# Attention stage of a hybrid encoder layer: bias tables made on chip from distances, an identity made on chip, a store cut into pairs, delta loads moved between stores

## What is computed

```
proj = rmsnorm(x) @ w_in                  # split in two halves of columns by the kernel
A: gated delta rule in chunks of 64 tokens, both directions; needs the inverse of
   I + lower (64 x 64 per chunk and head), whose 16 x 16 diagonal blocks are inverted first
B: windowed attention, 12 heads of 64 in 3 groups with dilation f = 1, 4, 16:
   scores[q, k] = q.k / 8 - slope[head] * |k - q| * f    where |k - q| <= 64 and in range
   scores[q, k] = -1e30                                  elsewhere
   then softmax and the weighted sum of v
x = x + w_out(gates of A and B);  x = x + 16 experts of SwiGLU;  y = rmsnorm(x)
```

## Time and profile before

| what | us |
|---|---|
| median of three runs | 2660.21 |
| the profiled execution, its own time | 2656.95 |
| its span in the trace | 2654.8 |
| token projection (first load to the last store's issue) | 483.8 to 924.0 |
| attention (first load to the last rows) | 931.8 to 1076.8 |
| delta rule, first load | 1090.1 |

### The profile page before, as it was taken

The page is one execution under the profiler, slowest core; times in us unless marked ns, Lnnn a source line. Parts: engine busy times, 40 slices in busy tenths (PEclk is TensorE's granted clock), DMA queues, the critical chain, the costliest instruction groups (busy, mean ns, idle before and its releaser), DMA issues. The chain is left out here.

```text
span 2654.8 us, 48695 instructions
## 1 busy us (share of the span) xinstructions
PE 2342.1 (88%) x20450; PEld 2093.9 (79%) x20450; DVE 1354.3 (51%) x1673; ACT 1076.3 (41%) x1584; POOL 380.7 (14%) x375
## 2 busy tenths in 40 slices
PE   3988899799999979698767999659999999999992
PEld 2766688689999868698763555349999999999992
DVE  4445411125454358233226543467777777777772
ACT  3555511011111048111126553136666666666662
POOL 0000000000000038454423220000001000100000
PEclk7999999899999979799988999869999999999996
DMA  3233331238666496554634431447777777777754
GB/s 113 56 83 83 91 133 73 77 108 252 208 193 181 135 248 175 151 138 130 218 115 149 142 126 66 158 150 275 270 247 275 270 258 267 262 264 268 259 163 176
DMA packets 180105, 465.10 MB, mean 175 GB/s; under 512 B 63312, under 2 KB 108016, under 8 KB 152128
## 3 DMA queue, kind: packets, MB, share of 16 engines
q1 hardware_dynamic: 166560, 414.51, 47.4%
q0 software_dynamic: 13344, 47.67, 6.4%
HBM read 363.76 MB, written 102.26 MB: 176 GB/s over the span
## 5 line engine op out<-in xcount | busy, mean ns | idle before, releaser
L78 DVE TENSOR_TENSOR ex_w_rest<-weights,ex_w_rounded 128x2048 fp32r<-128x2048 f32 x192 | 439.4, 2289 | 208.5 <-ACT ex_w_rounded L2286 206.7
L2286 ACT CAST ex_w_rounded<-weights 128x2048 fp32r<-128x2048 f32 x192 | 366.7, 1911 | 30.3 <-PEq L48 30.3
L85 PE MATMUL tk_acc<-tk_w_rounded,normed 128*128 128x336 f32 x800 | 257.9, 322 | 19.2 <-DVE tk_w_rest L78 19.2
L2180 PE MATMUL ex_g_acc<-ex_xt,ex_w_rounded 128*128 128x320 f32 x1024 | 272.4, 350 | 1.4 <-issue 1.4
L2180 PE MATMUL ex_u_acc<-ex_xt,ex_w_rounded 128*128 128x320 f32 x1024 | 271.0, 349 | 0.0
L85 PE MATMUL tk_acc<-tk_w_rounded,normed_rest 128*128 128x336 f32 x800 | 255.4, 319 | 0.0
L85 PE MATMUL tk_acc<-tk_w_rest,normed 128*128 128x336 f32 x800 | 255.1, 319 | 0.0
L2181 PE MATMUL ex_g_acc<-ex_xt,ex_w_rest 128*128 128x160 f32 x1024 | 242.8, 237 | 0.0
L2181 PE MATMUL ex_u_acc<-ex_xt,ex_w_rest 128*128 128x160 f32 x1024 | 241.6, 236 | 0.0
L2181 PEld LDWEIGHTS ex_g_acc<-ex_xt,ex_w_rest 128*128 128x128 f32 x1024 | 197.6, 193 | 0.0
L2181 PEld LDWEIGHTS ex_u_acc<-ex_xt,ex_w_rest 128*128 128x128 f32 x1024 | 195.9, 191 | 0.0
(11 more groups left out here) (291 smaller groups left out, 5126.8 us busy)
## 6 DMA issues: line engine op xcount, KB each, us to landing
weights<-in_w_expert SPq DMA_DIRECT2D x192, 1024.0 KB, 5.2
proj_tok<-tk_stage SPq DMA_DIRECT2D x10, 1680.0 KB, 8.3
laq<-sc_laq SPq DMA_DIRECT2D x20, 768.0 KB, 4.1
dl_la<-laq SPq DMA_DIRECT2D x20, 768.0 KB, 5.0
tk_w<-in_w_tok SPq DMA_DIRECT2D x10, 1344.0 KB, 6.3
ch_w<-in_w_ch SPq DMA_DIRECT2D x24, 512.0 KB, 4.0
sc_rows<-rows SPq DMA_DIRECT2D x40, 256.0 KB, 6.2
sc_qk<-qkv_ch SPq DMA_DIRECT2D x40, 256.0 KB, 6.8
```

Of the source, the lines that this page charges most:

```text
L78: return dve.tensor_tensor(out, whole, rounded.bitcast(F32), ALU.subtract)
L85: mm = pe.matmul(out, stationary[a], moving[b], start=(first and n == 0), stop=(last and n == len(pairs) - 1))
L2180: pe.matmul(bank[:, 0:2 * SLOTS], hi[:, cols], x.rearrange("p a n -> p (a n)"), start=first, stop=False, skip_group_check=True)
L2286: act.copy(w_hi[:, i % SPLIT], held[:, i % HELD]).then_inc(w_rounded, 1)
```

## The change

1. **Bias tables from distances.** The host gives 8 tables of distances, 128 x 256 (128 KB), in place of 8 bias tables of 128 x 1024. They go into a free part of the weight buffer. Each bias table is four products of its distances by a slope. ACT makes two of the four heads for tables 0, 6 and 7. POOL makes the other two of these, and all four of tables 2, 3, 5, 1 and 4. DVE waits for ACT's and POOL's parts, where it waited for a load.
2. **Identity on chip.** POOL clears the 80 x 4096 buffer and sets 16 diagonals, in place of the two broadcast loads. The negation goes: a constant of the stage before is given with its sign turned. POOL no longer waits for k, makes identity and tables first and then loads the `diag` pieces.
3. **Last token block by pairs.** Five transfers of 336 KB, each as soon as its two tiles are copied.
4. **Delta loads between stores.** SP stores tile 7 of the list, issues the delta loads that don't need the inversion, stores tile 8, waits for the inversion, loads the blocks, stores tile 9.

```diff
-        bias = sb("at_bias", [P, BIASES, GH * WIN])
+        distance = spare[:, HELD - 1].rearrange("p k c -> p (k c)").rearrange("p (n c) -> p n c", n=BIASES)
+        bias = sb("at_bias", [P, BIASES, GH, WIN])
...
                     for g in range(3):
-                        for n in range(BIASES):
-                            if first_use[n] == (t, g):
-                                sp.dma_start(bias[:, n], io["att_bias"][n]).then_inc(bias_loaded[n], 16)
+                        if t == 0:
+                            n = FIRST_TABLES[g]
+                            sp.dma_start(distance[:, n], io["att_distance"][n]).then_inc(distance_loaded[n], 16)
...
+                    if t == 0:
+                        for n in OTHER_TABLES:
+                            sp.dma_start(distance[:, n], io["att_distance"][n]).then_inc(distance_loaded[n], 16)
...
-                for stored_part, count in blocks_out:
-                    sp.wait_ge(stored_part, count)
-                delta_loads(sp)
-                for t in range(NT - LOADED_AHEAD, NT):
-                    store(t)
+                store(NT - 3)
+                begun.start(sp, io, dr)
+                store(NT - 2)
+                for blocks_stored, count in blocks_out:
+                    sp.wait_ge(blocks_stored, count)
+                begun.blocks(sp, dr)
+                store(NT - 1)
...
             def _(pool):
-                pool.wait_ge(qk_loaded[0][2], 32)
+                identities(pool)
+                for n in FIRST_TABLES:
+                    pool.wait_ge(distance_loaded[n], 16)
+                    for slot in range(2, GH):
+                        pool.tensor_scalar(bias[:, n, slot, :], distance[:, n], -slope_of(n, slot), None, ALU.mult).then_inc(bias_pool[n], 1)
+                for n in OTHER_TABLES:
+                    pool.wait_ge(distance_loaded[n], 16)
+                    for slot in range(GH):
+                        pool.tensor_scalar(bias[:, n, slot, :], distance[:, n], -slope_of(n, slot), None, ALU.mult).then_inc(bias_pool[n], 1)
...
                 invert(pool)
...
+                for n in FIRST_TABLES:
+                    act.wait_ge(distance_loaded[n], 16)
+                    for slot in range(2):
+                        act.activation(bias[:, n, slot, :], distance[:, n], ACT.Copy, scale=-slope_of(n, slot)).then_inc(bias_act[n], 1)
...
-                    dve.wait_ge(bias_loaded[n], 16)
+                    if n in FIRST_TABLES:
+                        dve.wait_ge(bias_act[n], 2)
+                        dve.wait_ge(bias_pool[n], GH - 2)
+                    else:
+                        dve.wait_ge(bias_pool[n], GH)
...
                 def store_block(c):
+                    if c == TOK_BLOCKS - 1:
+                        for pair in range(NT // 2):
+                            for parity in range(2):
+                                sp.wait_ge(copied[parity], NT // 2 * c + pair + 1)
...
+                        return
...
+    def identities(engine):
+        engine.memset(x[:], 0.0).then_inc(cleared, 1)
+        engine.wait_ge(cleared, 1)
+        for r in range(BLK):
+            engine.memset(x[:, :, r, :, r], 1.0).then_inc(diagonal_set, 1)
...
-            engine.dma_start(x[:, d].rearrange("p r q c -> p (r q c)"), io["blk_ident"].partition_broadcast(INV_P)).then_inc(loaded[n % AT_ONCE], 16)
...
-        engine.tensor_scalar(u[:], u[:], -1.0, None, ALU.mult).then_inc(negated, 1)
```

More of the change, by code:

```diff
@@ L506, in bias_of, with phase_attention @@
     return ((0 if t == 0 else 2 if t == TS // P - 1 else 1), 3 + t % 2, 5)[g]
-def phase_attention(nc, io, dr, ident, spare, delta_loads):
+def phase_attention(nc, io, dr, ident, spare, begun):
     with ExitStack() as ctx:
@@ L1237, in program @@
             engine.wait_ge(out[r], 16 * transfers(2 * len(parts), r))
-    return program, [(out[r], 16 * transfers(2 * len(parts), r)) for r in range(AT_ONCE)]
+    return identities, program, [(out[r], 16 * transfers(2 * len(parts), r)) for r in range(AT_ONCE)]
 RING = 4
```

89 lines of the change are left out of this document (53 added, 36 removed).

## The result

The changed kernel takes 2641.45 us (median of 14 runs, 2630.74 to 2652.22) where the kernel before, measured beside it, takes 2658.44 (14 runs, 2646.35 to 2666.73): ratio 0.995, 95% interval 0.9932 to 0.9968 (the two medians alone make 0.9936). A second measurement, further down, gave 0.9937 (0.992 to 0.9955). The forecast was 2637 us, range 2627 to 2649, and faster by over 0.5%: the time lies 4 us above the forecast, and the gain stands right at that bound, with the interval on both sides of it.

A forecast was written before the change was run, and what follows sets the result against it. It took experts, PE busy, to fill most of the span, with movable time between token stage and delta rule. Gains 2.8 + 10.0 + 0 + 8.7 = 21.5 us off 2656.95 gave 2635.5, or 2638.7 by median; forecast 2637, range 2627 to 2649.

The forecast's parts named there:

- Store by pairs: Handover from token stage to attention: last store issue to next transfer takes 4.9 us instead of 7.75, gaining 2.8 us.
- Units 0 to 4: First attention units: left where they were, shifted with the stage; gain 0, ends 1.5 us gained and 4 lost.
- the late start: Rival at POOL's first table: 7.0 us paid once make all units 4 us late; about 2641 us, chance 0.25.
- Units 4 to 13: Middle of the attention: units run at 3.874 us each once the transfer queue is relieved; 10.0 us gained, lower end nothing.
- both waits: In units 4 to 13, PE's 4.03 us for k of unit 9 and DVE's 3.66 us for tile 0's stores; both go.
- one pressure: Transfer queue in the attention: bias and identity loads together 4.4 MB less, near a third of the pressure from 938 to 990.
- Inversion: POOL's inversion in the attention stage: tables, diagonal loads, then 82.3 us as before; done at 1052.8 instead of 1069.9.
- Tail: Attention's end, last row to the delta rule's first load: 4.6 us in place of 13.3, gaining 8.7, ends 6 and 9.
- 11 us of slack: POOL's inversion against the last rows: it may end as late as 1064 instead of 1052.8 before it costs anything.
- the rivals with a cost: Attention start and POOL: the late start, and POOL becoming the bound through slow table heads (2683 us, chance 0.04).
- the middle stays clogged: Rival at units 4 to 13: unit 9 still waits, the clock falls, the 10 us stay away; about 2647 us, chance 0.14.
- the signs of being wrong: Attention: PE pausing for k or DVE for stores at units 8 to 12, late blocks, or tables delaying DVE beyond unit 3.

The follow-up runs named there:

- e2: Changed kernel with the last token block stored by one transfer after its last copy; median 2644.8 us, ratio to the kernel before 0.9927 to 0.997.
- e1: Changed kernel with SP's early delta loads put behind the inverse blocks, ahead of the last three tiles' stores; median 2649.3 us, ratio to before 0.9934 to 0.9977.
- e5: Changed kernel with the early delta loads issued sooner, behind the stores of tiles 3, 4 and 5; median 2631.5 us, ratio to before 0.9866 to 0.9933.
- e7: Changed kernel with PE kept busy across the change of stage by 12 and 18 unused products; median 2640.6 us, ratio to before 0.9904 to 0.9954.
- e9: e8 with 21 further unused products in PE's gaps early in the attention; median 2626.9 us, ratio to before 0.9862 to 0.9903.
- e11: e9 with four buffers for the rows instead of three; median 2625.3 us, ratio to before 0.9852 to 0.9902.
- e3: Changed kernel with the eight 512 KB biases loaded again instead of made from distances; median 2643.1 us, ratio to before 0.993 to 0.9965.
- e4: Changed kernel with the inversion's identity loaded by two transfers instead of set by POOL; median 2648.1 us, ratio to before 0.9955 to 0.9987.
- e8: Changed kernel with e5, e6 and e7 together; median 2631.1 us, ratio to before 0.9877 to 0.9938.
- e10: Changed kernel with e5 and e6 together, without products to keep PE busy; median 2635.5 us, ratio to before 0.9894 to 0.9934.
- e6: Changed kernel with POOL's diagonal loads issued between its last three tables instead of behind all; median 2635.8 us, ratio to before 0.9906 to 0.9948.

## Why the prediction was right, and where it was not

*Store by pairs.* Predicted 2.8 us, ends 2.0 and 3.8; measured 4.2, all of it this edit's (e2). The term was mis-sized: I took 4.9 us from the last issue to the next stage by leaning on the size of the store, and it was 3.53, below even the 4.0 of the small store at the attention's end.

*Units 0 to 4 and the late start.* Predicted 0; unit 4 began 24.38 us after the stage's start, where it was 24.90: right. The rival with a load paid once is refuted: six heads right behind the pool's configuration took 5.51 us, 852 ns busy each, and the twenty after them 848. The Trainium skill (GPSIMD Engine Reference, Instruction dispatch) gives some 6 us for the first call to a freshly loaded kernel; no such gap lies between this configuration, at 926.2 us, and the first head at 926.36.

*Units 4 to 13.* Predicted 10.0 us; measured 6.4 in the first trace, 69.81 - 24.90 - (65.52 - 23.66) = 3.1 in the second. In these two traces both waits and the second fall of the clock went, as argued; but only the wait for keys went for good. The stores of tile 0, which I had landed 44.4 us after the stage's start and 1 us before unit 9 wants them, landed at 45 to 49 us in e1, e2, e5 and e7, 1.1 to 2.0 us after unit 9 wanted them, and in e1 and e7 the clock fell again. The other step that failed is "Units 4 to 13 then run at 3.874": it took the clock to be at 1.00 from unit 4 because it was so in the one trace of before, and it can still be at 0.50 at unit 4 and unit 5. That the clock's rise is what is missing is shown by e9, where PE has no gaps, unit 5 begins 7 us earlier and from there the units run at 3.87 us each until the stores. My "upper end is also about 10" was too low a ceiling as well: from the stage's start, e11 reaches unit 13 at 55.03.

*Which loads did it.* I treated the 3.1 MB of biases and the 1.3 MB of the identity as one pressure. e3 and e4, one trace each, show that each alone puts 4 to 6 us back, at different places: the biases at the first units' keys, the identity at the stores of tile 1.

*Inversion.* The weakest step. Predicted done at 121.0 us from the stage's start (1052.8 in the frame of before), measured by 139.3: 18 us late. Of these, 3.3 are the tables (0.90 us a head for 0.75, just above the upper bound of 0.86), 3.7 the eight diagonal loads (17.7 us for 14), and 11.2 the step "then 987.6 to 1069.9 as before, 82.3 us": the steps took what they took, but the stores 34.2 us for 22.9. I had moved SP's early loads onto the very stretch in which POOL stores its blocks, and priced neither against the other; e1 (23.5 us) and e5 (25.6 us) show that collision. How much it costs varies: in the changed kernel's second trace SP reaches its early loads only at 122.3 us (117.7 in the first), and the sixteen issues take 22.3 us for 27.9. Nor is it the only thing that slows these stores: they took 25.0 us in e3, 25.0 in e8 and 27.1 in e10, where they went out earlier in the attention and beside no more than the four masks. What did it there, no run shows.

*Tail.* Predicted 8.7, measured 5.5 and, with later rows, 7.6. The 11 us of slack that I gave POOL were used up by its 18, and the blocks decided instead of the last rows. Where blocks are early the 4.6 us from last row to next stage are really 3.9 (e3, e5, e8 to e11); with the early loads issued just before them the last stores landed later (4.5 us in e6, 5.8 in the changed kernel's second trace).

*The sum.* 4.2 + 0.5 + 6.4 + 5.5 = 16.6 us for 21.5. In the second trace it is 15.7, with 3.1 of the middle and 7.6 of the tail. Nothing of it came from the rivals with a cost: no table held DVE up beyond unit 0 (which began 6.38 us after the stage's start, 1.8 us sooner than before), and POOL became the later chain only by a few us. Half of "the middle stays clogged" was true: e1 and e7 have the stores waited for and the clock falling. Of the signs of being wrong that the prediction names, two came in the first trace: the blocks landed after the last rows (139.26 for 138.12), and DVE paused for stores at unit 9, if only for 0.44 us. So the direction and the list of what pays were right, and the nearness of 2641 to 2637 is partly luck: 1.4 us more at the handover and 0.5 at units 0 to 4 stand against 6.8 less in the middle and the tail, and the range, 22 us wide, would have held the late start and the clogged middle as well.

## What to carry to other kernels

A gain in front of one chain is paid out only as far as the next chain allows: in the changed kernel the rows and the inverse blocks end within a few us of each other, so that the early clock of e2 and e7 brought the next stage forward by 0.6 and 0.3 us only, while clock, blocks and buffers together brought 11.8. When transfers are moved, put them down beside everything else that moves in the stretch they arrive in, on every queue; a stage's free stretch can be found in the windows' DMA share. And where a stage starts with the lower clock, don't take its length from one trace: read several, or give PE something to do in the gaps.

## What was not expected of the hardware

With the same instructions in the stage the granted clock rose 24 to 38 us after its start, and 32 or 38 us in two executions of one program, although PE was busy throughout from about 15 us on; unit 6 began at 31.9 us in e2 and at 38.3 in the changed kernel's second trace. A transfer of the same 160 KB took 3.4 us to land (median of 16) with SP's early loads behind it, and 5.9 and 4.3 in two executions of the changed kernel, which has them beside it (3.9 to 5.0 in e2, e4 and e7, which have them beside it too). And POOL's multiplication of a 128x256 table by a constant took 0.85 us, 3.3 ns an element, nearly four times its memset.
